# Two-layer trunk on one core: the first pair of both up-projections runs on x scaled per channel, and the norm's token factor is applied to its results

## What is computed

```python
def rmsnorm(x, g, eps=EPS):
    y = x32 * lax.rsqrt(jnp.mean(x32 * x32, axis=-1, keepdims=True) + eps) * g
...
def conv_ffn(h, w_up, w_dw, b_dw, w_down):
    a = causal_dwconv(h @ w_up, w_dw) + b_dw
    g, val = jnp.split(a, 2, axis=-1)
    return (jax.nn.silu(g) * val) @ w_down
...
        x = x + g1[:, None] * y
        h = rmsnorm(x, norm_g[layer, 1]) * (1.0 + sc2[:, None]) + sh2[:, None]
        x = x + g2[:, None] * conv_ffn(h, ff_w_up[layer], ff_w_dw[layer], ff_b_dw[layer],
                                       ff_w_down[layer])
```

## Time and profile before

| what | us |
|---|---|
| median of 3 runs | 1276.68 |
| lowest, highest | 1273.35, 1277.91 |
| the profiled execution's own time | 1277.44 |
| its span, first to last instruction | 1275.6 |
| PE busy in the span | 1244.9 (98%) |
| DVE, ACT, POOL busy | 704.9, 558.5, 530.5 |
| granted TensorE clock, mean | 0.977 of full speed |

### The profile page before, as it was taken

How to read it: one execution, slowest core, us unless ns; L and a number is a source line. 1 busy time by engine, 2 the same in 40 slices (tenths; PEclk the granted TensorE clock), 3 DMA queues, 4 the chain that set the end, 5 groups by cost and what they waited for, 6 DMA issues and landing times.

```text
span 1275.6 us, 17052 instructions
## 1 busy us (share of the span) xinstructions
PE 1244.9 (98%) x5558; PEld 992.6 (78%) x5558; DVE 704.9 (55%) x1161; ACT 558.5 (44%) x892; POOL 530.5 (42%) x265
## 2 busy tenths in 40 slices
PE   7999999989999999999999999999999999999996
PEld 6877777667888888888888777668788888888884
DVE  5557776763776733346887899972533333331002
ACT  4256656643533344442224655663544444442221
POOL 2243332132434444444452677734344444444440
PEclk7799999999999999999998999999999999999998
DMA  9943444221465522236673212103222222233321
GB/s 360 210 149 119 145 148 164 100 99 66 132 198 195 167 83 97 92 105 230 231 248 100 86 65 71 64 13 99 66 99 94 92 94 97 90 105 97 105 84 66
DMA packets 45639, 157.04 MB, mean 123 GB/s; under 512 B 5536, under 2 KB 5792, under 8 KB 45600
## 3 DMA queue, kind: packets, MB, share of 16 engines
q1 hardware_dynamic: 44928, 156.21, 37.0%
q10 hardware_dynamic: 672, 0.34, 0.1%
HBM read 154.10 MB, written 2.42 MB: 123 GB/s over the span
## 4 chain that ended last, share of the span: by engine, by line
PE 89%; DVE 5%; issue 2%; ACT 2%; DMA 1%; DVEq 0%; SPq 0%; ACTq 0%
PE psum L907 26%; PE psum L909 25%; PE psum L908 25%; PE psum L1238 3%; PE psum L918 1%; PE psum L941 1%; DVE psum L1476 1%; DVE pt_lo L1485 1%; PE psum L937 1%; PE psum L1067 1%; DVE acc L1324 1%; DMA ada_first<-ada_w 1%; PE psum L971 1%; PE psum L1094 1%; PE psum L1106 0%
## 5 line engine op out<-in xcount | busy, mean ns | idle before, releaser
L501 POOL TENSOR_TENSOR w_lo<-w_raw,w_hi 128x1024 fp32r<-128x1024 f32 (+1 forms) x192 | 455.6, 2389 | 689.8 <-ACT w_hi L586 689.8
L907 PE MATMUL psum<-h_hi,w_hi 128*128 128x512 f32 x1152 | 466.5, 405 | 4.0 <-DVE x L1580 2.2
L908 PE MATMUL psum<-h_lo,w_hi 128*128 128x512 f32 x1152 | 452.7, 393 | 0.0
L909 PE MATMUL psum<-h_hi,w_lo 128*128 128x512 f32 x1152 | 452.6, 393 | 0.0
L907 PEld LDWEIGHTS psum<-h_hi,w_hi 128*128 128x128 f32 x1152 | 219.2, 190 | 54.1 <-issue 7.3
L909 PEld LDWEIGHTS psum<-h_hi,w_lo 128*128 128x128 f32 x1152 | 218.7, 190 | 47.0
L908 PEld LDWEIGHTS psum<-h_lo,w_hi 128*128 128x128 f32 x1152 | 219.1, 190 | 46.0 <-issue 3.4
L586 ACT ACTIVATE w_hi<-w_raw 128x1024 fp32r<-128x1024 f32 (+1 forms) x192 | 195.7, 1032 | 87.4 <-DMA w_raw<-w_tiles 87.3
L907 PE MATMUL psum<-a_hi,w_hi 128*128 128x512 f32 x352 | 137.1, 389 | 1.1 <-issue 1.1
L908 PE MATMUL psum<-a_lo,w_hi 128*128 128x512 f32 x352 | 136.9, 389 | 0.0
L909 PE MATMUL psum<-a_hi,w_lo 128*128 128x512 f32 x352 | 136.9, 389 | 0.0
(11 more groups left out here) (187 smaller groups left out, 1353.2 us busy)
## 6 DMA issues: line engine op xcount, KB each, us to landing
w_raw<-w_tiles SPq DMA_DIRECT2D x160, 512.0 KB, 3.3
ada_buf<-ada_w SPq DMA_DIRECT2D x32, 512.0 KB, 3.4
w_raw<-w_tiles SPq DMA_DIRECT2D x32, 448.0 KB, 3.2
ada_late<-ada_w SPq DMA_DIRECT2D x28, 512.0 KB, 5.2
ada_mid<-ada_w SPq DMA_DIRECT2D x20, 512.0 KB, 4.5
ada_first<-ada_w SPq DMA_DIRECT2D x16, 512.0 KB, 10.1
x<-x_in SPq DMA_DIRECT2D x4, 512.0 KB, 7.1
bias<-rel_scratch SPq DMA_DIRECT2D x8, 256.0 KB, 10.6
```

The lines of the kernel that those rows point to most:

```text
L501: nc.gpsimd.tensor_tensor(w_lo[:, slot, 0:k], w_raw[:, (ph.tile + l) % 2, 0:k], f(w_hi[:, slot, 0:k]), ALU.subtract).then_inc(lo_done, 1)
L907: nc.tensor.matmul(dst, w_hi[:, slot, k], rhs_hi, start=first, stop=False)
L908: nc.tensor.matmul(dst, w_hi[:, slot, k], rhs_lo, start=False, stop=False)
L909: return nc.tensor.matmul(dst, w_lo[:, slot, k], rhs_hi, start=False, stop=last)
```

## The change

At both borders the first pair of `UP` no longer takes h. It takes g = x · gain, which needs no sum over the channels:

- `gain_early` computes the gain on DVE before `OUT` (and before `PW2`) starts.
- After each `residual` of two tiles, ACT copies each of them twice with the gain as scale (`gained`: to a PSUM bank and rounded to `g_hi`), and DVE subtracts into `g_lo`, ahead of its sum of the squares. `g_hi` and `g_lo` lie where the last eight tiles of `a_hi` and `a_lo` will.
- `gained_pair` on PE waits for `g_ready` by chunks, has `square_sum` behind its second chunk, and `keep_warm` is gone at these two borders.
- DVE multiplies the pair's two banks by the factor, of which ACT makes a second copy in SBUF (`scale_pair`, between the fourth and fifth tile of the norm); ACT adds the shift's column to them ahead of the taps. That column is sh2 @ W: POOL multiplies the two raw weight tiles by the shift, adds the eight chunks up in three steps, and PE multiplies the result by a column of ones (`shift_product`, behind the first chunk of the second pair).
- The weight tiles of the second pair are loaded only once POOL has read the raw tiles for that product. ACT rounds the first of them ahead of Ln, and the second behind the first `h_hi`. `turn` gives two banks in place of three at these norms.

```diff
-        a_lo_at = offset_of["a_lo"]
+        a_lo_at, a_hi_at = offset_of["a_lo"], offset_of["a_hi"]
+        g_hi = at("g_hi", [P, DK, S], F32R, a_hi_at + 4 * S * (FM - DK))
+        g_lo = at("g_lo", [P, DK, S], F32R, a_lo_at + 4 * S * (FM - DK))
+        w_shift = at("w_shift", [P, 2, DK, P], F32, a_hi_at + 4 * S * 4)
...
-            return psum[:, 4 + m % 3] if n else psum[:, FIRST_TURNS[m % 2]]
+            return psum[:, 4 + m % 3] if n == 2 else psum[:, FIRST_TURNS[m % 2]]
...
+            def load_first_up(ph, layer):
+
+                for l in range(4):
+                    if l >= 2:
+                        sp.wait_ge(shift_read, 2 * layer + l - 1)
+                    load_tile(ph, 0, l)
...
+            def first_up(ph, layer):
+
+
+                n = 1 + 2 * layer
+                for l in range(2):
+                    lo_tile(ph, 0, l)
+                shift = mod[:, SHIFT[n]:SHIFT[n] + DK].unsqueeze(2).to_broadcast([P, DK, P])
+                for l in range(2):
+                    nc.gpsimd.tensor_tensor(w_shift[:, l], w_raw[:, (ph.tile + l) % 2], shift,
+                                            ALU.mult).then_inc(shift_read, 1)
+                for l in range(2, 4):
+                    lo_tile(ph, 0, l)
+                pool.wait_ge(shift_read, 2 * (layer + 1))
+                for step, half in enumerate((4, 2, 1)):
+                    if step:
+                        pool.wait_ge(shift_step, 2 * layer + step)
+                    done = shift_sums if half == 1 else shift_step
+                    nc.gpsimd.tensor_tensor(w_shift[:, :, 0:half], w_shift[:, :, 0:half], w_shift[:, :, half:2 * half],
+                                            ALU.add).then_inc(done, 1)
...
                 for m in range(DK):
                     hi_of_h(n, m)
-                    if m == 2:
+                    if n in (1, 3) and m == 0:
+                        split_tile(then, 0, 3)
+                    if n in (1, 3) and m == 3:
+                        act.wait_ge(rms_ready, n + 1)
+                        nc.scalar.activation(rms[:], rms[:], ACT.Exp, scale=-0.5).then_inc(rms_copied, 1)
+                    if n == 2 and m == 2:
                         slots_free(then, 0, 1)
-                    if m in (2, 4):
+                    if n == 2 and m in (2, 4):
                         split_tile(then, 0, then.per_group + (m - 2) // 2)
...
+            def gained(n, i, c):
+
+
+                for m in range(4 * i + 2 * c, 4 * i + 2 * c + 2):
+                    at_ = DK * (n // 2) + m
+                    gain_col = gain[:, n, m:m + 1]
+                    if at_ >= 2:
+                        act.wait_ge(g_ready, at_ - 1)
+                    nc.scalar.activation(turn(n, m), x[:, m], ACT.Copy, scale=gain_col).then_inc(g_turned, 1)
+                    nc.scalar.activation(g_hi[:, m], x[:, m], ACT.Copy, scale=gain_col).then_inc(g_hi_done, 1)
...
                     squares(ph.bodies - 1, c, base, per_group)
+                    if n:
+                        gained(n, 1, c)
                     if then and c == 0:
                         split_group(then, 0, 0)
+                    elif n:
+                        slots_free(then, 0, 1)
+                        split_tile(then, 0, 2)
...
+                    elif c == 0:
+                        act.wait_ge(shift_mm, layer + 1)
+                        nc.scalar.activation(sm(W_SHIFT, 2), psum[:, SHIFT_BANK, 0:2], ACT.Copy).then_inc(shift_out, 1)
+                        act.wait_ge(shift_out, layer + 1)
+                        for j in range(2):
+                            act.wait_ge(scaled, 2 * layer + j + 1)
+                            nc.scalar.activation(psum[:, j], psum[:, j], ACT.Identity,
+                                                 bias=sm(W_SHIFT + j)).then_inc(whole, 1)
+                        act.wait_ge(whole, 2 * layer + 2)
...
+            def gained_pair(ph, n):
+
+
+                weights_ready(ph, 0, 0, 2)
+                pe.wait_ge(x_done, DK * (n - 1) + 6)
+                for k in range(DK):
+                    pe.wait_ge(g_ready, DK * (n // 2) + k + 1)
+                    for j in range(2):
+                        last = mm3(psum[:, j], j, k, g_hi[:, k], g_lo[:, k], k == 0, k == DK - 1)
+                    if k == 1:
+                        square_sum(n, 2)
+                last.then_inc(used, 1)
+
+            def shift_product(layer):
+
+                pe.wait_ge(shift_sums, layer + 1)
+                for j in range(2):
+                    last = nc.tensor.matmul(psum[:, SHIFT_BANK, j:j + 1], w_shift[:, j, 0], ones[:, 0:1],
+                                            start=True, stop=True)
+                last.then_inc(shift_mm, 1)
...
-            square_sum(1, 2)
-            keep_warm(18)
...
-            for c in range(2):
-                pair(UP0, 0, c, 2 * DK)
+            gained_pair(UP0, 1)
+            pair(UP0, 0, 1, 2 * DK, [lambda: shift_product(0)], 0)
...
-            square_sum(3, 2)
-            keep_warm(18)
-            pairs(UP1, 5 * DK, act_ready, FM, 1)
+            gained_pair(UP1, 3)
+            pair(UP1, 0, 1, 5 * DK, [lambda: shift_product(1)], 0)
+            pairs(UP1, None, act_ready, FM, 1)
...
+                if n in (1, 3):
+                    dve.wait_ge(g_ready, DK * (n // 2 + 1))
+                    norm_tiles(n, 0, DK // 2)
+                    scale_pair(n // 2)
+                    norm_tiles(n, DK // 2, DK)
+                    return
...
+                if ph in (OUT, PW2):
+                    for m in range(4 * i + 2 * c, 4 * i + 2 * c + 2):
+                        at_ = DK * (base // (2 * DK)) + m
+                        dve.wait_ge(g_turned, at_ + 1)
+                        dve.wait_ge(g_hi_done, at_ + 1)
+                        V.tensor_tensor(g_lo[:, m], turn(1, m), f(g_hi[:, m]), ALU.subtract).then_inc(g_ready, 1)
                 if not last:
                     add_group(i, c, base, per_group)
+
+            def scale_pair(layer):
+
+
+                dve.wait_ge(used, (UP0, UP1)[layer].group + 1)
+                dve.wait_ge(rms_copied, layer + 1)
+                for j in range(2):
+                    V.tensor_tensor(psum[:, j], psum[:, j], rms[:], ALU.mult).then_inc(scaled, 1)
...
+            gain_early(1)
             clear_sum(1)
...
+            gain_early(3)
             clear_sum(3)
```

44 lines of the change are left out of this document (31 added, 13 removed).

## The result

| | kernel before | changed kernel |
|---|---|---|
| median of the timed runs, us | 1277.04 (10 runs) | 1282.29 (10 runs) |
| lowest, highest | 1273.35, 1281.79 | 1278.67, 1286.49 |
| own time of the profiled execution | 1277.44 | 1284.44 |
| its span | 1275.6 | 1282.6 |

The changed kernel is slower: ratio 1.0042, 95% interval 1.0026 to 1.0059. That is 5.25 us, inside the predicted range, 2.8 us under the predicted time, and less than the 0.5% bound of the text: of the three classes it falls into "within 0.5%", which had 0.29, and not into "slower by over 0.5%", which had 0.64.

A forecast was written before the change was run, and what follows sets the result against it. PE was taken as the bound, with time to win only at the two borders. Terms 3.25 + 0.8 + 1.4 + 2 x 1.45 = 8.4 us on 1277.44 give 1285.8, less 0.76: 1285.1 us; range 1280 to 1289.5.

The forecast's parts named there:

- Part 4: Both borders: factor to third pair's weights takes 23.05 us, so the third pair starts 3.25 and 0.8 us later.
- Part 2: First output projection: new ACT copies and DVE subtractions delay the fourth pair's weights, a new PE wait of 2.85 us.
- Part 3: Last residual to norm factor, both borders: factor there at 324.95 (before 319.85) and 901.7; broadcast product taken as 2.42 us.
- Part 5: Half clock behind new waits: 1.4 us in the first output projection, 1.45 behind each wait ahead of a third pair.
- Rival B: Clock stays full, as each wait is split over moments with work around it: 4.05 us, 1280.7; chance 0.16.
- rival E: Broadcasts cost POOL twice the upper row, or DVE's conditioning pieces behind a later chain delay more: over 1289; chance 0.05.
- Rival C: Both borders: moved work on ACT, DVE and POOL stays hidden, PE runs through: 12.9 us faster, 1263.8; chance 0.07.

The follow-up runs named there:

- x3: Changed kernel with ACT rounding the third pair's weights among the norm's tiles, not behind the first pair's taps: 1279.35 us, ratio 1.0022.
- x1: Changed kernel with the first output projection's copies and subtractions for g behind its residuals, sums and fourth pair's weight rounding: 1279.91 us, ratio 1.0023.
- x2: Changed kernel with POOL's additions for the shift's column ahead of the second pair's weight subtractions: 1285.10 us, ratio 1.0068.
- x4: Changed kernel with nine small unused products by ones ahead of PE's wait for the shift's sum: 1283.72 us, ratio 1.0054.
- x5: Changed kernel with first output projection's copies late, third pair's weights early, POOL's shift additions ahead of second pair's weight subtractions: 1279.37 us, ratio 1.0022.
- x9: x5 with earlier sum of squares, second pair's weights behind Exp, earlier shift column, gated activation in SBUF, PE awaiting last tap: 1281.20 us, ratio 1.0026.
- x12: x9, but with the gated activation kept in SBUF in the second layer alone: 1272.92 us, ratio 0.9974 of the kernel before.
- x11: Kernel before without its warming products at the two borders: 1280.71 us, ratio 1.0026.
- x10: x9 without its SBUF move, with nine small products by ones behind each second pair: 1278.69 us, ratio 1.0004.

## Why the prediction was right, and where it was not

**Right.** The time, 1282.29, lies in the range (9.5 us wide), the sign is the forecast's, and the waits are where the text put them, ended by what it named: the fourth pair of the first output projection, the shift's sum and the third pair's weights at both borders. x3 shows that the chain of Part 4 decides (undoing it gives 2.9 us), x1 that Part 2's copies are the other term (2.4 us), x2 that the wait for the sum costs nothing of its own. That 5.25 us lie so well inside is in part luck: the clock's 4.3 us are missing, and 1.0 us came in behind the first border's third pair, which the sum did not have.

**Part 2, mis-sized.** The new wait is 3.39 us, forecast 2.85. ACT came at the time worked out; the surplus is POOL's two subtractions, 5.37 in place of 4.76, and it comes where DVE's two sums of squares fall beside them and not ahead of them: those take 3.48 in place of 1.42 in the profile of before. For the second output projection I counted nothing for the copies; the last residual comes 0.6 us later behind the first one (33.2 against 32.6).

**Part 3, near, by errors that partly cancel.** The product with a broadcast column is 1.9 us (3.75 for two), 0.5 below the 2.42 taken and inside the bounds; but at the second border POOL comes to it 1.3 us late, by the later residual and by subtractions of 5.43 in place of 4.75. The first border's factor is there at 326.01 where 324.95 was forecast, 0.46 of it run to run and 0.5 the longer wait above. The second border's is at 908.45, 6.2 us later than in the old time scale, so 902.3 against 901.7.

**Part 4, right.** From factor to third pair 22.6 us at both borders against 23.05: the norm's tiles 12.45 against 12.65, the two additions of the column 1.24 against 1.4, POOL 4.73 against 4.76.

**Part 5, the step that failed.** It put 4.3 us of clock on the path, 1.4 in the output projection and 1.45 behind each third pair's wait. In the profiled execution none of it is there: no fall in the output projection, and the falls at the borders stand behind the waits for the shift's sum (0.57 and 0.72 in the windows above), where they only shorten the wait for the weights. What the text took as the likely place, behind the third pair's wait, got a wait of 1.2 us and not of 3.6, and no fall. Part 5 did name the fall within the second pair; what it missed is that it can take the later one's place. Rival B's sum without the clock is 4.05 us, and up to the third pairs the two borders lose 3.4 + 0.9 = 4.3 in the profile. That B had the right arithmetic and the wrong reason is what the experiments add: the clock does fall. Behind the third pair's wait a fall cost 2.1 us at x2's second border, 1.8 at x4's and 3.0 in x1. Whether one falls in the output projection differs from profile to profile: in x2, x3 and x4, behind waits of 2.15, 3.56 and 2.19 us, the fourth pair takes 12.6 us, and in the changed kernel's profile, behind 3.39, 11.0. So the term of 1.4 there may be right in many executions, and the 2 x 1.45 behind the third pairs are what should have been nothing as long as the wait for the sum stands ahead.

**What the sum left out.** The 1.0 us behind the first border's third pair. The text has DVE's pieces of the conditioning only in rival E, with 0.05 together with the broadcasts. Their cover was 0.4 us before; with DVE's chain later it is gone.

**Rival C**, faster by 12.9 us, named one decisive point, the 23 us from factor to weights. x5 to x9 show that it was one of three: behind the weights stand the banks (x5: 4.48 us) and behind these, at the first border, the pieces of the conditioning (x9: 7.41 us). The removed 12.9 us could never have come out by the weights alone.

**Open.** The 1.3 us between the borders in the changed kernel's profile are put down to the stretch at half clock near 700 us; no run isolates it. What decides whether, where and how long the clock falls is not shown. That x12's gain lies at the second border is read from profiles and not timed apart.

## What to carry to other kernels

When work is moved in front of a serial step, the wait isn't removed but handed on: list what the engine needs next, in order (weights, banks, the next engine's side products), with the cover that each has in the profile, before counting a gain; here there were three gates within some microseconds, and each move paid only up to the next. Warming products paid where nothing behind them held PE (x11, some 3 us), and brought nothing measurable where PE met another wait (x4, x10); a wait that is left ahead of another wait is a cheap place for the clock to fall. Split a change by the place where it works: in the layer whose DVE had room it won, in the other it lost.
